# First attention with scores in three rounded passes, and values, reciprocals and row copies moved in the step

## The reference

```python
h = rms_norm(x, g_mix); z = h @ w_in
u, gb, gc, q, k, v = split(z)
y_conv = gb * short_conv(gc * u, conv_w)              # causal, width 3
q = rms_norm(q per head, g_q) * 64 ** -0.5            # k likewise with g_k
y_attn = dilated_mixture(q, k, v)                     # windows (128,1), (512,4), (2048,16)
mix = concat(rms_norm(y_conv), rms_norm(y_attn))
x = x + mix @ w_out
```

## Time and profile before

| | us |
|---|---|
| median of 3 runs | 3305.92 (3305.87 to 3307.49) |
| profiled execution | 3307.93 |
| its span | 3306.1 |
| TensorE busy | 3206.6 (97%) |
| VectorE, ScalarE, GpSimd busy | 1625.8, 1121.4, 993.9 |

### The profile page before, as it was taken

How to read it: one execution, slowest core, us unless ns; L and a number is a source line. 1 busy time by engine, 2 the same in 40 slices (tenths; PEclk the granted TensorE clock), 3 DMA queues, 4 the chain that set the end, 5 groups by cost and what they waited for, 6 DMA issues and landing times.

```text
span 3306.1 us, 52336 instructions
## 1 busy us (share of the span) xinstructions
PE 3206.6 (97%) x20620; PEld 2859.4 (86%) x20620; DVE 1625.8 (49%) x2700; ACT 1121.4 (34%) x2097; POOL 993.9 (30%) x688
## 2 busy tenths in 40 slices
PE   8999999999999999999999999999999999799997
PEld 6677768788888888999999899999999999799997
DVE  5554556755554545666666633155455043522223
ACT  3433333333322213555555531155455110300002
POOL 3112224787773333222222132200100222122222
PEclk9999999999999999999999999999999999799998
DMA  4000012122224112000000012100000221478888
GB/s 159 26 33 33 33 64 102 64 77 77 77 91 197 50 45 97 20 20 21 26 20 20 14 46 84 65 27 28 25 22 20 90 90 51 180 249 314 309 312 292
DMA packets 80582, 294.98 MB, mean 89 GB/s; under 512 B 11298, under 2 KB 16226, under 8 KB 77200
## 3 DMA queue, kind: packets, MB, share of 16 engines
q1 hardware_dynamic: 67296, 243.92, 20.3%
q0 software_dynamic: 6160, 18.63, 2.3%
q10 hardware_dynamic: 6944, 29.90, 2.3%
HBM read 239.39 MB, written 47.70 MB: 87 GB/s over the span
## 4 chain that ended last, share of the span: by engine, by line
PE 56%; DVE 2%; ACT 1%; issue 1%; DMA 0%; POOL 0%; SPq 0%; POOLq 0%; ACTq 0%; DVEq 0%
PE PS L657 14%; PE PS L3083 7%; PE PS L3536 7%; PE PS L645 5%; PE PS L3147 4%; PE PS L3566 4%; PE PS L3299 4%; PE PS L3114 3%; PE PS L3368 3%; PE PS L3333 3%; PE PS L3148 0%; PE PS L3096 0%; PE PS L3314 0%; PE PS L3369 0%; DVE affT L2936 0%
## 5 line engine op out<-in xcount | busy, mean ns | idle before, releaser
L679 POOL CAST w_hi<-ring 128x1024 fp32r<-128x1024 f32 x130 | 135.4, 1042 | 1563.5 <-PE PS L657 406.4
L681 POOL TENSOR_TENSOR w_lo<-ring,w_hi 128x1024 fp32r<-128x1024 f32 x130 | 332.6, 2558 | 10.4
L2214 ACT ACTIVATE EA<-EA,small_sb 128x1040 f32<-128x1040 f32 x144 | 166.6, 1157 | 186.3 <-DVE small_sb L2632 186.3
L2632 DVE CUSTOM_DVE_ANT_0 EA<-PS,biasH,low_a 128x1024 f32<-128x1024 f32 x128 | 163.6, 1278 | 57.8 <-PE PS L3114 57.8
L3083 PE MATMUL PS<-u_hi,w_hi 128*128 128x348 f32 x504 | 173.5, 344 | 0.0
L3083 PE MATMUL PS<-u_lo,w_hi 128*128 128x348 f32 x504 | 162.1, 322 | 0.0
L3083 PE MATMUL PS<-u_hi,w_lo 128*128 128x348 f32 x504 | 161.8, 321 | 0.0
L1610 DVE TENSOR_TENSOR hid_lo<-hid,hid_hi 128x1024 fp32r<-128x1024 f32 x44 | 91.9, 2128 | 118.7 <-ACT hid_hi L1252 118.7
L1702 PE MATMUL PS<-u_hi,w_hi 128*128 128x512 f32 x352 | 147.2, 418 | 3.0 <-POOL w_lo L681 2.3
L1899 PE MATMUL PS<-t_hi,slot_hi 128*128 128x512 f32 x352 | 138.7, 394 | 5.6 <-DVE t_lo L1511 4.0
L3147 PE MATMUL PS<-Va,PTa 128*128 128x128 f32 (+1 forms) x1152 | 139.9, 275 | 0.0
(11 more groups left out here) (489 smaller groups left out, 8323.8 us busy)
## 6 DMA issues: line engine op xcount, KB each, us to landing
ring<-in_stream SPq DMA_DIRECT2D x130, 512.0 KB, 3.3
w_gate_sb<-in_w_gate SPq DMA_DIRECT2D x64, 512.0 KB, 7.3
w_up_sb<-in_w_up SPq DMA_DIRECT2D x64, 512.0 KB, 7.3
w_down_sb<-in_w_down SPq DMA_DIRECT2D x64, 512.0 KB, 5.8
gu_raw<-in_gate_up SPq DMA_DIRECT2D x22, 1024.0 KB, 5.4
hid_keep<-hid_out SPq DMA_DIRECT2D x17, 512.0 KB, 2.9
hid<-hid_keep ACTq DMA_DIRECT2D x15, 512.0 KB, 16.2
x_keep<-xT ACTq DMA_DIRECT2D x1, 4176.0 KB, 14.7
```

The source lines that it names most:

```text
L679: pool.tensor_copy(w_hi[j][:, :, :], w_raw[j][:, :, :]).then_inc(S["w_rounded"], 1)
L681: pool.tensor_tensor(w_lo[j][:, :, :], w_raw[j][:, :, :], w_hi[j][:, :, :], ALU.subtract).then_inc(S["w_split"], 1)
L2214: act.activation(e[0:m, :], e[0:m, :], ACT.Exp, scale=-1.0, bias=small[0:m, 8 + 2 * par + k:9 + 2 * par + k], accum_out=small[0:m, 12 + 2 ...
L2632: dve.tensor_tensor_reduce(e[0:m, 0:T1], wide(2 * k, T1, m), bias, -1.0, low_a[0:m, t, k:k + 1], ALU.add, ALU.min, low).then_inc(S["aa_max ...
```

## The change

- The normalised k and q are kept raw in `yT1[:, pp]` and `convT[:, pp]` (both free until the pair's own results). ScalarE rounds them (`split_heads`), GpSimd subtracts for the remainders (`lower_heads`), into one buffer each of `k1_hi`, `k1_lo`, `q1_hi`, `q1_lo`. This goes by halves of 512 columns, for the next pair at s = 9.
- `scores` becomes three rounded passes of each head: hi hi, hi lo, lo hi. They wait for the remainders (`a1_kl`) at s = 0 and 4.
- TensorE issues `values(g - 1)` right behind `scores(g + 2)` in every step, and `turn_recips(g)` at the end of step g instead of in the middle of step g + 1.
- VectorE does `result(g - 1)` and `recip_rows(g)` ahead of `take_probs(g)`; ScalarE does `spread_recips(g - 1)` first in a step.
- GpSimd's loop over tile splits is written out, with `lower_heads` behind the tiles 3 and 4 and behind each pair's "b" tile.
- `first_tap` and `result` of tile 0 wait for `a1_kl`, since they write over the raw q and k.

```diff
-        kT1 = [o.put(f"kT1_{j}", [P, T1]) for j in range(2)]
-        qT1 = [o.put(f"qT1_{j}", [P, T1]) for j in range(2)]
+        k1_hi, k1_lo, q1_hi, q1_lo = (o.put(n, [P, T1], F32R) for n in ("k1_hi", "k1_lo", "q1_hi", "q1_lo"))
...
+        def raw_half(kind, pp, half):
+
+            return (yT1 if kind == "k" else convT)[:, pp, half * BANK:(half + 1) * BANK]
...
+                def lower_heads(pp, half):
+
+                    cols = slice(half * BANK, (half + 1) * BANK)
+                    for n, (kind, lo, hi) in enumerate((("k", k1_lo, k1_hi), ("q", q1_lo, q1_hi))):
+                        pool.wait_ge(S["a1_kh"], 4 * pp + 2 * half + n + 1)
+                        pool.tensor_tensor(lo[:, cols], raw_half(kind, pp, half), hi[:, cols], ALU.subtract).then_inc(S["a1_kl"], 1)
+
                 split_pair(0)
                 norm_split_odd(pool, 0, T1, u_hi, u_lo)
-                with pool.Fori(1, W_OUT0 // 2 + 1) as i:
-                    split_pair(i)
+                for n in range(2, W_OUT0 + 2):
+                    split(pool, n, n % 2, n // 2 + 1, n - 2)
+                    if n in (3, 4):
+                        lower_heads(0, n - 3)
+                    for pp in range(DCT - 1):
+                        if n == in_tile("b", pp):
+                            for half in range(2):
+                                lower_heads(pp + 1, half)
...
+                def split_heads(pp, half):
+
+                    cols = slice(half * BANK, (half + 1) * BANK)
+                    if pp:
+                        act.wait_ge(S["a1_s"], NS * pp)
+                    for n, (kind, hi) in enumerate((("k", k1_hi), ("q", q1_hi))):
+                        act.wait_ge(S["a1_qn"], 4 * pp + 2 * n + half + 1)
+                        act.activation(hi[:, cols], raw_half(kind, pp, half), ACT.Copy).then_inc(S["a1_kh"], 1)
...
                 def first_tap(pp, half):
                     act.wait_ge(S["conv_a"], 2 * pp + half + 2)
+                    act.wait_ge(S["a1_kl"], 4 * pp + 4)
...
                 root_halves("q", 0, 4)
+                split_heads(0, 0)
                 for half in range(2):
                     take_unit("u", 0, half)
+                split_heads(0, 1)
                 for a in range(2):
                     exp(0, a)
...
                     woven = woven_unit(pp, s)
+                    if g and chunks[(g - 1) % NS][1] == 0:
+                        spread_recips(NT * ((g - 1) // NS) + chunks[(g - 1) % NS][0])
...
-                    if g and chunks[(g - 1) % NS][1] == 0:
-                        spread_recips(NT * ((g - 1) // NS) + chunks[(g - 1) % NS][0])
                     if woven and woven[0] not in "cb":
                         take_unit(*woven)
+                    if pp + 1 < DCT and s == 9:
+                        split_heads(pp + 1, 0)
                     take_probs(g)
                     if g + 2 < DCT * NS and (g + 2) % NS in last_chunk.values():
                         for a in range(2):
                             exp(NT * ((g + 2) // NS) + chunks[(g + 2) % NS][0], a)
+                    if pp + 1 < DCT and s == 9:
+                        split_heads(pp + 1, 1)
...
+                    if t == 0:
+                        dve.wait_ge(S["a1_kl"], 4 * pp + 4)
                     dve.wait_ge(S["a1_rb"], n + 1)
...
+                    if g and (g - 1) % NS in last_chunk.values():
+                        result(g - 1)
+                    if chunks[s][1] == 0:
+                        recip_rows(g)
                     take_probs(g)
                     if g + 2 < DCT * NS:
                         scores(g + 2)
-                    if chunks[s][1] == 0:
-                        recip_rows(g)
-                    if g and (g - 1) % NS in last_chunk.values():
-                        result(g - 1)
...
-                    if s == 0:
-                        pe.wait_ge(S["a1_qn"], 4 * pp + 4)
+                    if s in (0, HALF):
+                        pe.wait_ge(S["a1_kl"], 4 * pp + (4 if s else 2))
                     if g:
                         pe.wait_ge(S["a1_max"], 2 * g)
-                    for a in range(2):
-                        r = slice(a * HD, (a + 1) * HD)
-                        last = mm(bank(a, k1 - k0), qT1[pp % 2][r, t * P:(t + 1) * P], kT1[pp % 2][r, k0:k1], start=True, stop=True)
+                    for n, (q, keys) in enumerate(((q1_hi, k1_hi), (q1_hi, k1_lo), (q1_lo, k1_hi))):
+                        for a in range(2):
+                            r = slice(a * HD, (a + 1) * HD)
+                            last = mm(bank(a, k1 - k0), q[r, t * P:(t + 1) * P], keys[r, k0:k1], start=(n == 0), stop=(n == 2))
...
                     if g + 2 < DCT * NS:
                         scores(g + 2)
+                    if g:
+                        values(g - 1)
                     if s == 0 and g:
-                        values(g - 1)
                         turn_values(pp)
                     turn_probs(g, 0)
-                    if g and chunks[(g - 1) % NS][1] == 0:
-                        turn_recips(g - 1)
                     if woven and late:
                         unit(*woven, 0)
                     if woven:
                         unit(*woven, 1)
                     turn_probs(g, 1)
-                    if s:
-                        values(g - 1)
+                    if chunks[s][1] == 0:
+                        turn_recips(g)
```

More of the change, by code:

```diff
@@ L484, in build @@
             conv_u conv_a conv_t conv_k conv_y mix_sq mix_acc cn_sum cn_sd cn_r cn_n cn_hi cn_lo an_sum an_sd an_r
-            a1_u a1_raw a1_sq a1_ss a1_sc a1_sd a1_r a1_qn a1_vf a1_vt a1_vs a1_s a1_max a1_e a1_t a1_pt_d a1_pt_a a1_o a1_y a1_rd a1_rl a1_rt a1_rb a1_acc
+            a1_u a1_raw a1_sq a1_ss a1_sc a1_sd a1_r a1_qn a1_kh a1_kl a1_vf a1_vt a1_vs a1_s a1_max a1_e a1_t a1_pt_d a1_pt_a a1_o a1_y a1_rd a1_rl a1_rt a1_rb a1_acc
             a1_ysq a1_yn a1_hi a1_lo a1_lo_odd wo_x op_g op_t op_hi op_lo rs_b
@@ L997, in take_raw @@
                     i = norm_index(kind, pp)
-                    raw = (qT1 if i % 2 else kT1)[pp % 2][:, half * BANK:(half + 1) * BANK]
+                    raw = raw_half(kind, pp, half)
                     gain = g_heads[:, G_Q8:G_Q8 + 1] if i % 2 else gains[:, G_K:G_K + 1]
```

## The result

The changed kernel takes 3325.37 us (median of 5 runs, 3320.7 to 3329.8) against 3305.87 us: 1.0057 times as long, 95% interval 1.0044 to 1.0071. The forecast of slower was right; its 3316 us and its range, up to 3323 us, were too low. The difference is +19.5 us, not +10.8.

What follows compares the result with a forecast made beforehand. TensorE work was taken to bound most steps, VectorE's chain pair 3's tail. Terms -3.1 - 3.6 + 10.5 + 2.2 + 0.4 + 1.0 + 3.4 = +10.8 us on the median 3305.92 gave 3316 us, range 3302 to 3323.

Steps and rivals of the forecast that it cites:

- Scores, -3.1 us: First attention's scores: three rounded passes instead of float32 save 0.15 us per 512-column score; -3.1 us, bounds 0 and -5.
- Values behind scores, -3.6 us: Values issued right behind scores save an array-mode entry, 0.1 us in each of 36 steps; bounds 0 and -7.
- The stall at s = 4, +10.5 us: Values at s = 4 wait for ScalarE's reciprocal copy: 3.0 us in pairs 0 to 2, 1.5 us in pair 3.
- s = 0, +2.2 us: At s = 0 the score waits 0.75 us for VectorE's maximum, no longer covered by values, three times.
- Clock, +3.4 us: Two of three new TensorE holes at s = 4 bring half clock, 1.7 us each; bounds 0 and +7.
- Rival (a): The stall at s = 4 comes but no lower clock: 3313.3 us, chance 0.22.
- Tail, +1.0 us: End of pair 3: VectorE's early result, sum and row copy delay the next score's maximum; bounds -3 and +3.
- Rounding and remainders, 0: Added ScalarE rounding copies and GpSimd subtractions fit in those engines' free time and cost nothing.
- (d): Rival: GpSimd's split late at pair boundaries, scores of s = 0 wait 3.4 us three times: 3326 us, chance 0.06.
- (e): Rival: passes of two heads not side by side, 0.7 us more per wide chunk: 3330 us and more, chance 0.02.
- (b): Rival: no stall at s = 4 and no gain lost: 3303 us, chance 0.18.
- (c): Rival: faster, as VectorE runs ahead where it bounds and the stall stays under 1 us: 3299 us, chance 0.10.

Runs made afterwards that it cites:

- e14: The changed kernel with constant matmuls before the values at s = 4 and before the reciprocals' transpose at s = 6 of pairs 0 and 3: 3317.16 us.
- e13: As e10, with 15 pairs of constant matmuls in pair 0's hole, ahead of the transpose of the reciprocals: 3298.52 us, 0.9983 of before.
- e10: The changed kernel with ScalarE's reciprocal copy at the end of the same step and one late GpSimd split held back: 3303.81 us.
- e5: The changed kernel with constant matmuls (12, in pair 3 6) in the hole before the values at s = 4: 3317.74 us.
- e3: The changed kernel with ScalarE's reciprocal copy moved to the end of the same step, behind its probability copy: 3305.72 us, 1.0002 of before.
- e7: The changed kernel with VectorE's sum put back behind the maximum, result and row copy left in front: 3321.34 us.
- e6: The changed kernel with the early reciprocal copy and, in the last six steps, the order of before on all engines: 3302.68 us.
- e4: The changed kernel with the order of before on all engines in the last six steps (pair 3, s = 6 to 11): 3314.43 us.
- e9: The changed kernel with GpSimd's split of the output projection's second tile waiting for the maximum of score 10 of pair 3: 3317.78 us.
- e11: The changed kernel with 18 constant matmuls ahead of score 9 of pair 3: 3323.59 us.

## Why the prediction was right or wrong

e14 has the waits of the changed kernel. e13 has not those for the copy (but 0.67 us) nor that for GpSimd, and keeps the others. Neither has half clock between score 0 of pair 0 and score 11 of pair 3. Behind it e14 has 10.2 us and e13 3.4, and e14 is 2.3 us longer there, by the copy, the clock or both. So 411.01 - 396.76 = 14.3 us is about what these waits cost. 420.18 (or 422.23) - 411.01 = 9.2 (or 11.2) us is what the lower clock adds on top of e14; 1.8 (2.1) of it is the old half clock of pair 0, which the kernel before had too (score 9 to 10: 7.18 or 7.51 us against 5.40).

- **Scores, -3.1 us: right.** 0.90 us start to start (0.91 said), 0.16 us less a wide score; alone -3.3 us by the medians and -1.3 in the stretch, which cannot be told from none. A whole pass saved in each wide chunk, some 6 us, was not borne out. (By proportion to the columns the passes' 0.235 us give 0.12 and 0.08 us at 384 and 256 columns, not the 0.10 and 0.04 of the sum; that is 0.1 us a pair.)
- **Values behind scores, -3.6 us: right in sign, too small.** Step by step the early copy against rounding alone gives a further 0.18 us in wide steps (7.73 to 7.55, 8.16 to 7.97) where I took 0.1. Rounding and move together save 103.85 + 0.56 - 101.74 = 2.7 us a pair, 2.1 said.
- **The stall at s = 4, +10.5 us: right.** 2.9 us each in pairs 0 to 2 of e14 against e13 (86.60, 104.65 and 104.62 us against 83.72, 101.75 and 101.73); in pair 3 score 6 to 7 takes 12.92 us against 11.39, 1.5 us: +10.2.
- **s = 0, +2.2 us: right, a little large.** Score 1 to 2 of a pair 6.13 us against 5.57, three times, +1.7. **s = 1, 2, +0.4: right.** Score 4 to 5 of pair 3, 8.37 against 7.97, as said.
- **Clock, +3.4 us: right where I looked, and not looked far enough.** At s = 4 two falls of 1.6 and 1.4 us in the first execution and three of 1.6 in the second. The price was worked out; that there would be two was a guess. Rival (a), no fall, is out.
- **Tail, +1.0 us, bounds -3 and +3: the step that failed; +7.5.** With its hole filled (e14) the tail takes 50.42 us, so 4.3 of the 7.5 us are the clock and 3.2 the waits. By part:
  - Score 8 to 9 costs 2.2 more: 1.4 for VectorE standing behind GpSimd (5.95 to 4.55 with GpSimd held), 0.8 for the rest of the order. I had a row with the long sum in the earlier trace rows and put 1.0 to 2.4 us on it as a length that varies, without asking what it waited for.
  - Score 9 to 10 costs 2.75 more, all of it half clock (7.41 us against 4.02 at full, where before took 4.66): I had put falls at s = 4 alone, though the clock of 0.89 in the earlier trace rows says that the tail of before was at half clock for 6.8 us already (from 448.12 and 461.78, 3.41 us each). The prediction took the hole of 1.2 us at 443.33 for harmless; a half clock begins 4.8 us behind it, and whether the hole had a part in it no run shows.
  - Score 10 to 11 is equal (before had half clock there itself).
  - From score 11 to the output projection 2.5 more: the values of tile 7's first chunk stand 2.56 us for the copy, which now lies behind two roundings of the convolution (474.10 to 476.0). That is the mechanism of s = 4 again, at s = 11, where the roundings stand on ScalarE ahead of the copy as the roots do at s = 4; I went through s = 0, 1, 2, 4 and not the last steps. With the early copy the same wait is 0.67 us and this part takes 32.66 us in place of 34.44, so 1.8 of the 2.5 us are the copy's, with the half clock behind its hole; the other 0.7 are not located, and with rounding alone, in the order of before, this part takes 33.60. The lines are of ScalarE and TensorE of e10:

```profile
454.52 0.27 ACT L1107 ACTIVATE r_cols<-PS 128x128 f32<-128x128 f32 x1
...
454.85 1.92 PE L1826 MATMUL PS<-PT,V 128*64 128x128 f32 x16 [0.67 <-ACT r_cols L1107]
```

- **Rounding and remainders, 0: right.** No score waits for a remainder; (d) and (e) did not happen, nor did (b) and (c).
- **Pair 0, steps 6 and 7, 0: a little wrong.** Score 8 to 9 takes 8.07 us against 7.33, and 7.86 with the sum late: +0.7.

In the second execution: +10.2 + 1.7 + 0.4 + 4.7 (three falls) + 7.5 = 24.5, and the stretch is 17.1 longer, so the savings are 7.4 us, against 6.7 forecast. That sum is not free of doubt in pair 0, whose old hole had half clock in both. The direction and the stall were forecast for the right reason. Of the 8.7 us by which the forecast was short, 6.3 lie in the stretch, where the tail alone is 6.5 over its term; the other 2.4 lie outside it, where nothing was changed, and no run explains them. What stays open: why e5, whose profiled stretch is 4 to 6 us shorter, has a median 7.8 us lower; why e3 has two groups of times; and what sets the half clock behind the stretch, 65 to 85 us between executions of kernels that are equal there. Executions of one kernel lie up to 11 us apart (e13), which limits what medians can tell.

## What to carry to other kernels

When work is moved ahead in one engine's order, look up the place of what it waits for in the producer's own order, at every step of the loop, the last ones too: a copy that now lay behind other work of its engine cost more (10.2 us) than the cheaper matmuls and the move gave (7.4 us). Price a new hole on TensorE at its length plus what the half clock behind it costs (1.4 to 1.6 us each here), most of all where the trace has half clock already, and put filler into the hole itself, ahead of the instruction that waits. A row with an odd duration may be a wait: see what the other engines do at its end.

## What the runs showed of the hardware

- Two kinds of VectorE instructions stand while GpSimd's subtraction of 1024 columns runs, and end with it: the sum of two SBUF operands, 2.08 us against 0.28, and the row copy from SBUF to SBUF, 1.23 against 0.23. Others next to it do not: the result with one PSUM operand took 0.29 us (447.07 in after), and the reciprocal from SBUF to SBUF 0.17 us (448.37 in e7). With the order of before (e6) the probability copy and the maximum, which read PSUM, ran beside it in 0.69 and 0.68 us. So it is not every instruction on SBUF that stands. The Trainium skill (SBUF — State Buffer, Who interferes with whom) states such a rule: a VectorE instruction with two SBUF inputs contends with a GpSimd instruction that reads SBUF, a copy in a two-port mode contends with GpSimd too, and the one that issues second is blocked until the first is done. The sum agrees; in which mode the row copy ran no run shows. The rule points at 1.4 us of the tail's 2.2 in score 8 to 9, and not at the clock or the late copy.
- A hole of 2.8 us ahead of dense matmuls brought 3.41 us at 1.2 GHz in five of six cases at s = 4 of pairs 0 to 2, at 1.4 to 1.6 us each. With e4, e7, e9 and e11, which have the same hole, it is 15 of 18; the three without are all in pair 0. Filled with matmuls on constants, never in six (e5, e14).
- Cheaper scores need not save time where TensorE already waits: the tail took 47.28 us with rounding alone, 47.22 before.
